# Gated delta pairs on one core: masks by selection on GpSimd, and a new order of copies, splits and decay products

## The reference

```
# gated DeltaNet, per chunk and direction
decay = where(incl, exp(g_i - g_j), 0)
L     = where(strict, (k beta) k^T * decay, 0)      # then a solve with (I + L)
intra = where(incl, q k^T * decay, 0)
o     = rms_norm(o, norm_g) * silu(zgate)
# mLSTM
w     = exp(log_w - m_t) * q k^T                    # log_w is -inf outside incl
h     = h + concat(y_rw, y_gd, y_ml) @ w_out
```

## Time and profile before

| what | us |
|---|---|
| median of three runs | 3547.33 |
| lowest, highest | 3545.54, 3583.12 |
| profiled execution | 3570.83 |
| its span, first to last instruction | 3568.7 |
| mean granted TensorE clock | 0.950 of full speed |
| TensorE busy | 3288.6 (92%) |
| VectorE busy | 2127.9 (60%) |
| ScalarE busy | 1676.7 (47%) |
| GpSimd busy | 555.3 (16%) |

### The profile page before, as it was taken

One profiled execution on the slowest core, in us unless ns is written; L12 is line 12 of the kernel. 1 busy time (PEld: TensorE's weight loads), 2 busy tenths in 40 slices (PEclk: granted clock), 3 DMA queues, 4 the chain that ended last, 5 costly groups with the idle time before them and its releaser, 6 DMA issues.

```text
span 3568.7 us, 56178 instructions
## 1 busy us (share of the span) xinstructions
PE 3288.6 (92%) x19578; PEld 2911.5 (82%) x19578; DVE 2127.9 (60%) x3373; ACT 1676.7 (47%) x2565; POOL 555.3 (16%) x431
## 2 busy tenths in 40 slices
PE   6999788888899999999989997888888999999998
PEld 6999687777688888888789996787777888888876
DVE  4565445667677777544455653546765777775544
ACT  5444534344555555444454444433436555554443
POOL 2000221244022222100000002213440222220000
PEclk9999778899999999999999997889989999999999
DMA  5456100111455555555555660001115555555553
GB/s 175 148 173 187 36 1 1 58 48 48 131 187 188 186 184 190 183 195 176 174 164 157 183 188 1 1 1 58 59 47 161 189 189 190 190 181 201 193 191 136
DMA packets 263085, 477.39 MB, mean 134 GB/s; under 512 B 16988, under 2 KB 80280, under 8 KB 261720
## 3 DMA queue, kind: packets, MB, share of 16 engines
q1 hardware_dynamic: 262872, 474.63, 41.5%
HBM read 472.47 MB, written 2.10 MB: 133 GB/s over the span
## 4 chain that ended last, share of the span: by engine, by line
PE 76%; DVE 10%; issue 4%; ACT 4%; DVEq 2%; DMA 1%; POOL 1%; ACTq 1%; POOLq 1%; SPq 0%
PE ps L550 76%; DVE Z L1535 1%; DVE wlo L1512 1%; ACT L1100 1%; DMA ring<-in_w_ple_gate_dram 1%; ACT YB L1100 1%; DVE TN L1578 1%; ACT whi L1100 1%; DVE XS L1568 0%; DVEq L1537 0%; DMA ring<-in_w_in_dram 0%; ACT Z L1100 0%; POOL wlo L486 0%; DVE heads L1597 0%; DVE upair L1525 0%
## 5 line engine op out<-in xcount | busy, mean ns | idle before, releaser
L1512 DVE TENSOR_TENSOR wlo<-ring,whi 128x1024 fp32r<-128x1024 f32 (+4 forms) x902 | 1124.2, 1260 | 840.6 <-ACT whi L1100 835.8
L550 PE MATMUL ps<-upair,whi 128*128 128x512 f32 (+1 forms) x5248 | 1429.5, 344 | 23.0 <-DVE wlo L1512 19.3
L1100 ACT ACTIVATE whi<-ring 128x1024 fp32r<-128x1024 f32 (+4 forms) x944 | 944.0, 1004 | 1054.4 <-PE ps L550 965.5
L550 PE MATMUL ps<-upair,wlo 128*128 128x256 f32 x4032 | 1135.6, 282 | 0.0
L550 PEld LDWEIGHTS ps<-upair,whi 128*128 128x128 f32 x5248 | 910.3, 190 | 150.1 <-DVE wlo L1512 21.7
L550 PEld LDWEIGHTS ps<-upair,wlo 128*128 128x128 f32 x4032 | 767.3, 190 | 0.0
L550 PE MATMUL ps<-whi,upair 128*128 128x390 f32 (+2 forms) x1280 | 362.9, 362 | 2.0 <-DVE wlo L1512 2.0
L550 PE MATMUL ps<-whi,ghi 128*128 128x512 f32 x704 | 274.7, 390 | 2.6 <-DVE wlo L1512 2.6
L550 PE MATMUL ps<-whi,glo 128*128 128x512 f32 x704 | 274.0, 389 | 0.0
L550 PE MATMUL ps<-wlo,ghi 128*128 128x512 f32 x704 | 274.0, 389 | 0.0
L550 PEld LDWEIGHTS ps<-whi,upair 128*128 128x128 f32 x1280 | 237.2, 188 | 24.4 <-DVE wlo L1512 3.1
(11 more groups left out here) (285 smaller groups left out, 3767.4 us busy)
## 6 DMA issues: line engine op xcount, KB each, us to landing
ring<-in_w_up_dram SPq DMA_DIRECT2D x352, 512.0 KB, 3.7
ring<-in_w_down_dram SPq DMA_DIRECT2D x176, 512.0 KB, 4.3
ring<-in_w_in_dram SPq DMA_DIRECT2D x128, 384.0 KB, 3.6
ring<-in_w_out_dram SPq DMA_DIRECT2D x64, 512.0 KB, 3.5
ring<-in_w_ple_gate_dram SPq DMA_DIRECT2D x64, 512.0 KB, 4.4
ring<-in_w_in_dram SPq DMA_DIRECT2D x64, 390.0 KB, 3.2
ring<-in_w_in_dram SPq DMA_DIRECT2D x48, 512.0 KB, 4.4
ring<-in_w_in_dram SPq DMA_DIRECT2D x32, 396.0 KB, 3.9
```

What stands on the lines that cost most here:

```text
L550: return pe.matmul(o_, a, b, start=start, stop=stop, skip_group_check=True)
L1100: return act.activation(o_, i_, f, **kw)
L1512: v.tensor_tensor(wlo[:, slot % RING, :, 0:w], ring[:, slot % RING, :, 0:w], whi[:, slot % RING, :, 0:w].bitcast(F32), SUB).then_inc(S["lo ...
```

## The change

Seven edits. The masks of the gated delta decays and of the mLSTM weights are made by affine_select on GpSimd, each behind a 128x1 product and ahead of a drain; negstrict is gone, and its sign moves into VectorE's strict product. GpSimd's split of a stage's first slot waits for gd_ss of the stage before instead of gd_ssq, and the second slot's waits for the stage's first gd_arg. TensorE makes the decays in four groups, strict ones of direction 0 first, and waits for the copy of the last chunk only behind that group; gd_gb counts four a stage. ScalarE copies chunk 3 ahead of the norm, except in the last stage. In the last stage VectorE splits slot 24 ahead of head_out, GpSimd adds the last two chunks only when the turned output's low part is ready, and TensorE turns the output ahead of its wait for the last copy.

```diff
--- before.py
+++ after.py
@@ -149,7 +149,6 @@
         ones = sb("ones", [P, P])
         headones = sb("headones", [P, P])
         incl = [sb(f"incl{d}", [P, P]) for d in range(2)]
-        negstrict = [sb(f"negstrict{d}", [P, P]) for d in range(2)]
         LEVELS = 7
         lev = [sb(f"lev{d}", [P, LEVELS, P], BF16) for d in range(2)]
         pred = [sb(f"pred{d}", [P, 4, P], BF16) for d in range(2)]
@@ -432,8 +431,6 @@
                     sel(early, early, ALU.is_ge, lo + b - 1, [[2 * b, nb], [0, b]], -1)
                     pool.drain()
                     sel(lev[d][:, m, :], lev[d][:, m, :], ALU.not_equal, 0, [[-1, P]], 1, 1.0)
-            for d in range(2):
-                pool.tensor_tensor(negstrict[d][:], ident[:], incl[d][:], ALU.subtract)
             pool.drain().then_inc(S["masks"], 1)
 
             with pool.Fori(0, DEPTH) as L:
@@ -496,14 +493,17 @@
                     sg = pool.snap(base + i * OUT_SLOTS)
                     ng = pool.snap(L * (GP * NO) + i * NO)
                     if i:
-                        pool.wait_ge(S["gd_ssq"], L * GP + (i + 1))
+                        pool.wait_ge(S["gd_ss"], L * GP + i)
                         split_lo(sg, SL_OUT)
+                        pool.wait_ge(S["gd_arg"], pool.snap(n * 2) + 1)
                         split_lo(sg, SL_OUT + 1)
-                    for j, mask in enumerate((negstrict, incl)):
+                    for j in range(2):
                         for d in range(2):
+                            step, cm = ((1, -1), (-1, 1))[d]
                             pool.wait_ge(S["gd_d"], pool.snap(n * 2) + (2 * d + j + 1))
-                            pool.tensor_tensor(scores[d][:, j, :, :], scores[d][:, j, :, :], bmid(mask[d][:], 4),
-                                               ALU.mult).then_inc(S["gd_dm"], 1)
+                            pool.tensor_tensor(pst[:, 0:1], ident[:, 0:1], ident[:, 0:1], ALU.mult)
+                            sel(scores[d][:, j, :, :], scores[d][:, j, :, :], ALU.is_ge, j - 1, [[0, 4], [step, P]], cm)
+                            pool.drain().then_inc(S["gd_dm"], 1)
                     pool.wait_ge(S["inv_tn1"], pool.snap(L * (2 * (RC + GP)) + (i * 2 + 2 * RC)) + 2)
                     if i:
                         add_partial(ng, -2)
@@ -516,14 +516,16 @@
                     split_lo(sg, SL_OUT + 5)
                     split_lo(sg, SL_OUT + 6)
                     for d in range(2):
+                        step, cm = ((1, -1), (-1, 1))[d]
                         pool.wait_ge(S["ml_d"], n + (d + 1))
+                        pool.tensor_tensor(pst[:, 0:1], ident[:, 0:1], ident[:, 0:1], ALU.mult)
                         dg = ml_diag(d)
                         for h in range(2):
-                            pool.tensor_tensor(dg[h], dg[h], bmid(incl[d][:], 2), ALU.mult)
+                            sel(dg[h], dg[h], ALU.is_ge, 0, [[0, 2], [step, P]], cm)
                         pool.drain().then_inc(S["ml_dm"], 1)
                     split_lo(sg, SL_OUT + 7)
                     add_partial(ng, 1)
-                pool.wait_ge(S["gd_done"], L * GP + GP)
+                pool.wait_ge(S["yt_ready"], L * 8 + (2 * GP + 2))
                 add_partial(ng, 2)
                 add_partial(ng, 3)
 
@@ -933,18 +935,25 @@
                     for j, bank in enumerate((7, 5)):
                         last = mm(ps[bank][:, :], ones[:], mono(KB[j][:, :, :], 2), True, True)
                     last.then_inc(S["gd_ssq"], 1)
-                    if i:
-                        pe.wait_ge(S["wo_evac"], L * (GP * NO) + NO * i)
-                    for d in range(2):
+                    def decays(d, j):
                         for h in range(2):
                             for t in range(NT):
                                 o_ = slice((2 * h + t) * P, (2 * h + t + 1) * P)
                                 lg = gs[:, 0 + 2 * t + d, h:h + 1].to_broadcast([P, P])
                                 lb = gs[:, 4 + 2 * t + d, h:h + 1].to_broadcast([P, P])
-                                mm(ps[2 + d][:, o_], lg, incl[d][:], True, True)
-                                mm(ps[4 * d][:, o_], lg, incl[d][:], True, False)
-                                last = mm(ps[4 * d][:, o_], lb, ident[:], False, True)
+                                if j:
+                                    last = mm(ps[2 + d][:, o_], lg, incl[d][:], True, True)
+                                else:
+                                    mm(ps[4 * d][:, o_], lg, incl[d][:], True, False)
+                                    last = mm(ps[4 * d][:, o_], lb, ident[:], False, True)
                         last.then_inc(S["gd_gb"], 1)
+
+                    decays(0, 0)
+                    if i:
+                        pe.wait_ge(S["wo_evac"], L * (GP * NO) + NO * i)
+                    decays(0, 1)
+                    decays(1, 0)
+                    decays(1, 1)
                     if i == 0:
                         ml_back()
                     pe.wait_ge(S["gd_rn"], n + 1)
@@ -1014,8 +1023,8 @@
                     for s in range(6, OUT_SLOTS):
                         out_slot(i, s)
 
+                turn_out(GP)
                 pe.wait_ge(S["wo_evac"], L * (GP * NO) + GP * NO)
-                turn_out(GP)
                 for s in range(OUT_SLOTS):
                     out_slot(GP, s, [(2 * i, 2 * i + 1) for i in range(NO)])
 
@@ -1411,10 +1420,13 @@
                             act.wait_ge(S[src], n2 + (d + 1))
                             a(mono(dst[d][:, :, :], 2), ps[4 * d][:, lo:lo + T], ACT.Copy).then_inc(S[done], 1)
                     split_out(sg, lg, 9)
+                    if i < GP - 1:
+                        partial_out(ng, sg, 3)
                     act.wait_ge(S["gd_ss"], n + 1)
                     rsqrt(st[:, 2, :], st[:, 1, :], 1.0 / P, epsb[:, 0:1]).then_inc(S["gd_rstd"], 1)
+                    if i == GP - 1:
+                        partial_out(ng, sg, 3)
                     split_out(sg, lg, 10)
-                    partial_out(ng, sg, 3)
 
                 turned_out(act.snap(L * 8 + 2 * GP))
                 for i in range(NO):
@@ -1906,7 +1918,7 @@
                     m2 = v.snap(L * (2 * (RC + GP)) + (i * 2 + 2 * RC))
                     n4 = v.snap(n2 * 2)
                     def exponents(d, j):
-                        v.wait_ge(S["gd_gb"], n2 + (d + 1))
+                        v.wait_ge(S["gd_gb"], n4 + (2 * d + j + 1))
                         for h in range(2):
                             for t in range(NT):
                                 u = 2 * h + t
@@ -1918,8 +1930,11 @@
                         v.wait_ge(S["gd_dm"], n4 + (2 * j + d + 1))
                         for h in range(2):
                             pp = ps[6 + h][:, :].rearrange("p (t j c) -> p t j c", t=2, j=2)
-                            v.tensor_tensor(scores[d][:, 2 + j, 2 * h:2 * h + 2, :], pp[:, :, j, :],
-                                            scores[d][:, j, 2 * h:2 * h + 2, :], MUL)
+                            o_, mask = scores[d][:, 2 + j, 2 * h:2 * h + 2, :], scores[d][:, j, 2 * h:2 * h + 2, :]
+                            if j:
+                                v.tensor_tensor(o_, pp[:, :, 1, :], mask, MUL)
+                            else:
+                                v.scalar_tensor_tensor(o_, pp[:, :, 0, :], -1.0, mask, MUL, MUL)
 
                     def products():
                         for d in range(2):
@@ -1991,14 +2006,15 @@
                     if i < GP - 1:
                         gd_prepare(i + 1)
                     head_squares("gd", OT)
+                    if i == GP - 1:
+                        v.wait_ge(S["lo_ready"], sl + (RING + SL_OUT + OUT_SLOTS * GP))
+                        split_lo(sl, SL_OUT + OUT_SLOTS * GP, SL_OUT + OUT_SLOTS * GP + 1)
                     head_out(i, n, "gd", lambda h: bmid(gdn[:, :], 2),
                              lambda t: zgt[:, t, ds(i * T, T)].rearrange("p (h c) -> p h c", h=2), RW)
 
                 v.drain().then_inc(S["mixp_free"], 1)
 
 
-                v.wait_ge(S["lo_ready"], sl + (RING + SL_OUT + OUT_SLOTS * GP))
-                split_lo(sl, SL_OUT + OUT_SLOTS * GP, SL_OUT + OUT_SLOTS * GP + 1)
                 turned_out(v.snap(L * 8 + 2 * GP))
                 split_lo(sl, SL_OUT + OUT_SLOTS * GP + 1, SL_OUT + OUT_SLOTS * GP + AHEAD)
                 v.wait_ge(S["wo_added"], L * (GP * NO) + (GP * NO + 2))
```

## The result

| kernel | median us (lowest to highest, runs) | to the kernel before [95% interval] |
|---|---|---|
| before, beside it | 3554.7 (3542.6 to 3583.1, 19) | |
| changed | 3542.0 (3521.3 to 3558.7, 19) | 0.9945 [0.9923, 0.9968] |

The ratio is that of the means, 3540.3 and 3559.7 us: the change makes the kernel 0.55% faster, by 19.4 us, and by the interval 11 to 27 us; the two medians differ by 12.7. Forecast were 18.1 us, 0.51%. All of this is within the 1% that the prediction called no change. The profiled execution has a span of 3529.0 us, 39.7 less than before's, so I first asked how much of that the change can have made.

A forecast was written before the change was run, and what follows sets the result against it. Bound by the chain of waits, TensorE holding 76%, VectorE 10%. Steps 5.6 + 6.6 + 1.0 + 2.2 + 2.7 = 18.1 us, taken from the median 3547.3, give 3529 us; range 3512 to 3553.

The forecast's parts named there:

- C's clock: Crossings between pairs: TensorE's score products at 1.2 GHz in all four, where one escapes today; minus 1.8 us.
- Step A: mLSTM masks: selections of about 0.41 us replace GpSimd's products, TensorE's level 4 wait falls from 2.12 to 1.2; 5.6 us.
- rival 3: mLSTM diagonal blocks: selections cost 0.90 us, deciding from 0.65, and TensorE's idle grows; 10 us slower, 3557 us; chance 0.05.
- Step B: TensorE's clock behind the level 4 wait: four of five falls to 1.2 GHz go with the shorter idle; 6.6 us.
- rival 1: Level 4: the clock still falls behind the shorter wait; saving 11.5 us, 3536 us; chance 0.27.
- Step C: Four crossings between pairs: open table load, norm 1.6 us later, AR done 0.7 us sooner; 2.8, with the clock 1.0 us.
- Rival 2: Crossings: the table load stays hidden, placed ahead of the copies; AR 1.25 us sooner, saving 23 us, 3524 us; chance 0.12.
- Step D: Masks of the scores: 0.45 us twice in a layer's pair 0, 1.3 us at the later identity additions; 2.2 us.
- Step E: Layer's end, twice: VectorE's split moves into the norm wait, last quarter starts 1.35 us earlier, chunk additions hidden; 2.7 us.

The follow-up runs named there:

- end_undone: Changed kernel with the layer's end as before (VectorE's slot 24 split behind the last norm, GpSimd's additions at gd_done); 3544.4 us, one run.
- ml_mult: Changed kernel with only the mLSTM masks back at GpSimd's multiplications; 0.9968 to the kernel before, median 3543.4 us in 10 runs.
- copy_behind: Changed kernel with ScalarE's copy of chunk 3 behind the norm's inverse root again; 0.9940 to the kernel before, 3534.0 us in 6 runs.
- only_ml: Kernel before with one edit, the mLSTM masks by selection; 0.9971 to the kernel before, median 3543.6 us in 12 runs.
- gd_mult: Changed kernel with the masks of the scores back at one multiplication each, without the 128x1 product and drain; 3547.1 us, one run.
- wait_long: Changed kernel with three more 128x1 products and drains on GpSimd ahead of the first direction's mLSTM mask, lengthening TensorE's level 4 wait; 3540.2 us.
- wait_long2: Second execution of the changed kernel with three more 128x1 products and drains ahead of the first direction's mLSTM mask; 3542.7 us.
- v2: Changed kernel with ScalarE's order norm, copy, inverse norms, and GpSimd's second split behind the first mask and third exponents; 0.992 to before, 3527.0 us in 6 runs.

## Why the prediction was right, point by point

The saving came out at 19.4 us by the means, with an interval of 11 to 27, for a forecast of 18.1. The time itself was 3542.0 us for 3529: 7.4 of the 13 us lie in the start, since the forecast began at a median of three runs, 3547.3, and nineteen gave 3554.7. The mean over two executions of before gives 18.4 us for the parts that the change reaches. The terms, by the first execution of before, against what the prediction put:

| step | forecast | pieces of the trace |
|---|---|---|
| A, mLSTM masks | 5.6 | 5.3 (wait 12.7 to 7.5) |
| B, falls in level 4 | 6.6 | 7.4 (102.4 to 95.0); 2.8 against the second execution |
| C, crossings, without the clock | 2.8 | 2.5 (56.0 to 53.4) |
| D, ahead of the first stages | 0.9 | 1.9 (two waits, 8.90 to 7.05) |
| C's clock and the rest of D | -1.8 + 1.3 = -0.5 | 2.6 (223.3 to 220.7); 0.0 against the second |
| E, layer end | 2.7 | 3.9 (45.5 to 41.6) less 1.4 behind the last quarter's start: 2.5; 1.6 against end_undone |

**Step A** held: the selection took 0.39 us where 0.41 was put between its neighbours of 128 and 512 columns, and rival 3, which wanted 0.65 and more, fell with that. In a layer's first stage the wait stayed at 1.35.

**Step B** held in direction, and rival 1 (the falls stay) fell: 0 of 54 with the short wait. Its size was read from one profile, which had five falls of six; the same kernel's second execution had two. By the mean of the two step B is 5.1 us, and by all stages with a long wait (10 of 30, two in a run) it is 3. That a part of the saved wait comes back as a longer low stretch at the scores (ml_mult) was in no step.

**Step C** held in mechanism: the open table load, the norm 1.65 us later (1.6 put), the inverse norms at 10.47 us as the wait that took the old one's place (820.45 less 810.02 = 10.43 put), and the crossing at 13.2 and 13.5 (13.3 put). Rival 2 fell with the load at 792.82. copy_behind shows it from the other side: the order of before, with the rest of the change, is 1.1 to 1.2 us a crossing better. For the clock I put 1.8 us in all, for one crossing's scores. All four crossings do have their score products at 3.78 us; but the low level also goes on behind them, and each of the six stages holds 5.4 to 7.0 us of it. What this cost is known only roughly: from the scores to the wait the changed kernel takes 2.3 us more than only_ml (220.7 for 218.4), in one execution of each, and no less than before's second execution.

**Step D** was right in one half and wrong in the other. Ahead of a layer's first stage gd_mult gives the wait back in full, 0.93 us, where I had put 0.45: I had taken AR to be held by the selection for 0.78 us, and it was not held at all. The other half, 1.3 us behind the identity addition, did not come: the idle there is gone with either mask. gd_mult also finds 0.63 us a crossing, which stood inside my step C.

**Step E** was sized on a slower turn. Before, the eight turns of the layer's end took 1.97 us (the row of before is below), and I kept ScalarE's high parts at the times that this gave; after, the same turns take 1.09 in both layers. Where a variant with the change's end has them at 1.96 or 1.97 (wait_long, wait_long2, ml_mult, the second layer of v2), the piece from the states to the last quarter is 21.5 us, 1.25 less than before's and near the 1.35 put; with turns of 1.09 it is 20.8, 1.95 less. With the old end it is 22.74 to 22.86 by either turn, since VectorE's held split bounds it. What failed is the sentence that the two chunk additions "are hidden" behind ylo. They are over before the residual sums, but VectorE waits 2.28 us for the second, and the MLP's turns come 33.3 us behind the last quarter's start in all ten executions with the change's end, where end_undone has 32.05. That gives back 1.2 to 1.3 us a layer; left are 0.8 against end_undone and 1.1 to 1.2 against before, for 1.35 put.

```profile
898.97 1.97 PE L554 MATMUL ps<-ident,YB 128*128 128x128 f32 x8 [3.47 <-DVE YB L1604]
```

For a mean execution B was put some 1.5 us too large, D's first half 1 us too small, its second half is absent, and E's two errors, a gain too small and a loss put at nothing, offset each other in part; the 1.8 us put against C for the clock do not show against before. The total is nearer than its parts, and that is luck in part; with an interval of 11 to 27 us the runs alone could not have told a saving of 12 from it.

## What to carry to other kernels

A wait saved on a TensorE that is nearly always busy paid here in two ways, in itself and in the clock behind it, and the second can move to another place: count the time at the low level over the whole stage before and after, not only behind the wait. Work moved out of the way of one path has to be followed to the next place where something waits for it: the chunk additions behind ylo helped to bring the last quarter forward by 2.05 us and gave 1.2 to 1.3 of them back at the residual sums, 9 us behind its start. A share of falls read from one profile is one draw; the same kernel gave five of six and two of six. Before moving work ahead of an activation that needs another table, see whether the load was hidden in the wait there: here the copy ahead took 1.1 us off one path and put 1.3 us of load on the one that ends.

## What the runs showed of the hardware

Two selections on GpSimd over 128x256 fp32 took 0.78 us beside VectorE reading PSUM, two products 1.43; over 128x512 one took 0.63 alone and 0.83 beside AR's two-input products in a crossing. Ahead of a layer's first stage it took 1.99 beside all four of them, and there AR was not held (0.40 us each), while a product as the mask, begun 0.2 us ahead of AR, held it for 1.33. I had not expected how far a stretch at 1.2 GHz shifts when work a third of a stage away is moved: at the score products of the changed kernel it went on for some 2 us behind them, in ml_mult it ended with them, and in v2 it was not there. Nor that some 17.5 us of a profiled difference of 39.7 can come from stretches whose instructions are the same.
